# Linear attention: the dense block beside the scan in pieces of four rows at every second step, not two rows at each

## What is computed

```python
def step(s, inp):                       # one chunk of one direction
    qc, kc, vc, gc = inp
    b = cumsum(gc, axis=-2); b_last = b[..., -1:, :]
    qb = qc * exp(b); kb = kc * exp(-b)
    a = where(mask, qb @ kb.T, 0.0)
    o = qb @ s + a @ vc
    kd = kc * exp(b_last - b)
    return exp(b_last) * s + kd.T @ vc, o
# 256 context and 256 latent tokens: 8 chunks, forwards and backwards
# finish: y = (rms_norm(o_forward + o_backward) * silu(r)) @ w_out,   r = h @ w_r
```

## Time and profile before

| | |
|---|---|
| time of three runs | 2943.78, 2946.37, 2949.68 us (median 2946.37) |
| span of the profiled execution | 2941.8 us (the page gives no time beside the span) |
| TensorE busy | 2857.8 us, 97% |
| VectorE busy | 1846.1 us, 63% |
| ScalarE busy | 1144.0 us, 39% |
| GpSimd busy | 323.7 us, 11% |
| scan of layer 0, heads 0 to 2 | 819.2 to 910.8 us of the span |
| scan of layer 3, heads 0 to 2 | 2613.4 to 2703.5 us of the span |

### The profile page before, as it was taken

The page is one execution under the profiler, slowest core; times in us unless marked ns, Lnnn a source line. Parts: engine busy times, 40 slices in busy tenths (PEclk is TensorE's granted clock), DMA queues, the critical chain, the costliest instruction groups (busy, mean ns, idle before and its releaser), DMA issues.

```text
span 2941.8 us, 43541 instructions
## 1 busy us (share of the span) xinstructions
PE 2857.8 (97%) x18470; PEld 2331.1 (79%) x18470; DVE 1846.1 (63%) x2673; ACT 1144.0 (39%) x1646; POOL 323.7 (11%) x290
## 2 busy tenths in 40 slices
PE   9999999999999999999999999999999999998999
PEld 8888888997955788877667887876778878774899
DVE  4477776557465576755876676557556765546554
ACT  3345565444254422233244222344442223334443
POOL 1000003011002201111011101200111002000110
PEclk9999999999999999999999999999999999999999
DMA  8947324554211345432213444330134443221353
GB/s 295 332 136 258 129 101 158 187 187 175 99 44 40 147 158 186 172 115 101 71 45 133 182 172 158 129 112 30 44 139 176 174 156 129 102 72 44 131 185 130
DMA packets 59618, 406.76 MB, mean 138 GB/s; under 512 B 6520, under 2 KB 9848, under 8 KB 11168
## 3 DMA queue, kind: packets, MB, share of 16 engines
q1 hardware_dynamic: 58224, 399.74, 37.4%
q0 software_dynamic: 1200, 4.23, 0.5%
HBM read 402.34 MB, written 1.09 MB: 137 GB/s over the span
## 4 chain that ended last, share of the span: by engine, by line
PE 86%; DVE 8%; ACT 3%; issue 2%; POOL 1%; DVEq 0%; ACTq 0%; POOLq 0%
PE bank L626 25%; PE bank L628 24%; PE bank L627 24%; DVE xnlo L2570 1%; DVE part L2579 1%; DVE wlo L2104 1%; PE bank L732 1%; PE bank L1138 1%; PE bank L1188 1%; PE bank L1300 1%; PE bank L1282 1%; PE bank L1266 1%; PE bank L1132 1%; ACT whi L1394 1%; PE bank L1142 1%
## 5 line engine op out<-in xcount | busy, mean ns | idle before, releaser
L2104 DVE TENSOR_TENSOR wlo<-raw,whi 128x2048 fp32r<-128x2048 f32 (+2 forms) x260 | 591.4, 2274 | 410.5 <-ACT whi L1394 410.2
L1394 ACT CAST whi<-raw 128x2048 fp32r<-128x2048 f32 (+2 forms) x260 | 487.8, 1876 | 633.4 <-PE bank L628 627.6
L626 PE MATMUL bank<-xnhi,whi 128*128 128x512 f32 (+2 forms) x1760 | 657.7, 374 | 19.2 <-DVE xnlo L2570 9.8
L628 PE MATMUL bank<-xnhi,wlo 128*128 128x512 f32 (+2 forms) x1760 | 646.3, 367 | 0.0
L627 PE MATMUL bank<-xnlo,whi 128*128 128x512 f32 (+2 forms) x1760 | 644.9, 366 | 0.0
L626 PEld LDWEIGHTS bank<-xnhi,whi 128*128 128x128 f32 (+1 forms) x1760 | 332.0, 189 | 117.5 <-issue 50.0
L628 PEld LDWEIGHTS bank<-xnhi,wlo 128*128 128x128 f32 (+1 forms) x1760 | 332.3, 189 | 56.8 <-issue 0.7
L627 PEld LDWEIGHTS bank<-xnlo,whi 128*128 128x128 f32 (+1 forms) x1760 | 332.6, 189 | 54.3 <-issue 0.9
L626 PE MATMUL bank<-hidhi,whi 128*128 128x512 f32 (+1 forms) x1024 | 373.6, 365 | 0.0
L628 PE MATMUL bank<-hidhi,wlo 128*128 128x512 f32 (+1 forms) x1024 | 372.2, 364 | 0.0
L627 PE MATMUL bank<-hidlo,whi 128*128 128x512 f32 (+1 forms) x1024 | 371.3, 363 | 0.0
(11 more groups left out here) (354 smaller groups left out, 4134.2 us busy)
## 6 DMA issues: line engine op xcount, KB each, us to landing
raw<-in_wall SPq DMA_DIRECT2D x317, 1024.0 KB, 4.8
vraw<-in_wall SPq DMA_DIRECT2D x60, 1024.0 KB, 4.8
x<-in_x SPq DMA_DIRECT2D x2, 1024.0 KB, 6.8
bias<-relative_offsets POOLq DMA_DIRECT2D x2, 768.0 KB, 7.1
x<-relative_offsets POOLq DMA_DIRECT2D x2, 768.0 KB, 9.1
out<-x SPq DMA_DIRECT2D x1, 1024.0 KB, 4.8
aqk<-aqk POOLq DMA_DIRECT2D x2, 256.0 KB, 3.3
cst<-in_cst SPq DMA_DIRECT2D x1, 492.0 KB, 10.6
```

The lines of the kernel that those rows point to most:

```text
L626: mm(out, wh, xh, start=first, stop=False)
L628: return mm(out, wl, xh, start=False, stop=last)
L1394: nc.scalar.copy(b.whi[u % SPL][:, rows, cols], b.raw[pos % RAW][:, rows, cols]).then_inc(*R.made("hi_ready"))
L2104: ttn(b.wlo[u % SPL][:, rows, cols], b.raw[blocks[u] % RAW][:, rows, cols], b.whi[u % SPL][:, rows, cols], ALU.subtract).then_inc(*R.made( ...
```

## The change

`slow_unit` gives way after every fourth row, and the scan asks for a piece in steps 1, 3, 5 and 7 only:

```diff
@@ slow_unit
                 if k == KC - 1:
                     last.then_inc(*R.made("chunk_ready"))
                     g["chunks"] += 1
-                if k % 2:
+                if k % 4 == 3:
                     yield
@@ gla, end of a step
-                next(beside, None)
+                if s % 2:
+                    next(beside, None)
                 if ahead and s == 3:
                     gate_input(h + 1, 1)
```

## The result

Ten runs of the changed kernel gave 2951.39 to 2956.62 us, median 2954.83; ten of the kernel before 2943.78 to 2949.68, median 2946.32. The medians are 8.5 us apart; the ratio is 1.0027 [1.0020, 1.0035], which is 8.0 us with an interval of 5.9 to 10.3. So the change costs about 8 us. The forecast was 2955.7, in a range of 2947.5 to 2962.5. The profiled execution went from a span of 2941.8 to 2949.6, +7.8. That is near the forecast's +9.3, but it is not made up as forecast: layer 0 gave what the sum said, layer 3 did not.

The account below looks back on a forecast made before the run. TensorE's queue bounds layer 0; in layer 3 the chain passes between TensorE, VectorE and ScalarE. Layer 0's +5.1 and layer 3's +4.2 make +9.3 us; on the median 2946.37 that gives 2955.7, range 2947.5 to 2962.5.

Parts of the forecast that it names:

- -0.20 - 0.43: Layer 0: steps 4 and 5 save 0.20 us by joining pieces; L1078 of step 7 comes only its slack, 0.43, earlier.
- the price that the last head had shown: Layer 0, L1138 of step 1: with no piece in step 0 it waits 0.26 us, as in the piece-free last head.
- The step of the argument that carried it: Layer 0, step 3: L2647 stays put, so L1078 gains only its slack; step 7: L2647 shifts with TensorE, slack 0.43 us.
- One small term: Layer 0, steps 0 and 1 together: 0.26 us of wait less 0.20 for the join, about +0.06.
- the plain join: Layer 0: a piece leaving an even step saves 1.58 us, joined to the next adds 1.38; without new wait -0.20.
- The rival that had only joins: VectorE's decay rows come earlier, so only 24 joins count: -4.8 us (2941.6), or -9.6 at double worth; chance 0.10.
- The two prices of 0.70: Layer 3, each head: six more matmuls behind L1078 of steps 3 and 7 cost 0.70 us each, 4.2 in all.
- I take both as cancelling: Layer 3 at 1.2 GHz: step 3's 0.70 us becomes up to 1.40, but step 4 profits from its missing piece.
- the prediction's own last sign of being wrong: Layer 3 off by more than 3 us through the low-clock stretches; heads 0 to 2 were forecast at 94.3 us.
- the rival with the clock that comes back sooner: Layer 3: dense matmuls behind L1078 shorten the low stretches, two heads gain 2.74 us each: +3.8, 2950.2; chance 0.18.
- What was said against it: Against the sooner clock, layer 3: the idle before step 3 gets longer by about a piece.
- The deeper clock: Layer 3: second head's low stretch lengthens (+2.74 us), step 7 gains one per head (5.1): +17.1, 2963.5; chance 0.12.

Follow-up runs that it names:

- the run with steps 0 and 4 emptied: Kernel before, both layers, with the pieces of steps 0 and 4 moved to steps 1 and 5: 2941.82 us, ratio 0.9984 to the kernel before.
- the two kernels with three fillers: Kernel before and changed kernel, each with idle matmuls added in layer 3 (three in heads 0 to 2, one in last): 2937.90 and 2946.80 us.
- the run in layer 3 alone: Kernel before with the change's moved pieces in layer 3 only, layer 0 left as it was: 2947.27 us, ratio 1.0004 to the kernel before.
- the two halves: Kernel before with the change in layer 0 only, 2952.04 us (ratio 1.0016), and in layer 3 only, 2947.27 us (ratio 1.0004).
- the change with two fillers: Changed kernel with two matmuls into an unused bank at the end of step 2, layer 3, heads 0 to 2: 2948.02 us, ratio 1.0009.

## Why the prediction was right, and where it wasn't

**Layer 0 came step by step as forecast.** The starts of L1068 and L1078 in the two timelines:

| layer 0 | before | changed | moved | forecast |
|---|---|---|---|---|
| L1068 to L1078 of step 3, first head | 12.41 | 11.47 | -0.94 | -1.00 |
| the same, second head | 13.19 | 13.05 | -0.14 | -0.15 |
| L1078 of step 3 to the next L1068, first head | 2.80 | 4.17 | +1.37 | +1.38 |
| on to L1078 of step 7, first head | 12.37 | 11.72 | -0.65 | -0.20 - 0.43 |
| on to the next head's L1068, first head | 2.79 | 4.17 | +1.38 | +1.38 |

The first head is +1.16 (forecast 1.13), the second +1.92 and the third +1.93 (1.98), together 5.0 for 5.1. L1138 of step 1 waits 0.26, the price that the last head had shown. The waits at step 7 are 1.1 (1.2 was named), that at step 3 of the second head 0.97. The step of the argument that carried it, that VectorE's L2647 doesn't come earlier when TensorE does, held: in step 7 it came just as much earlier as its slack said, and not more. One small term was not consistent: 0.06 was taken off the first head's slack and not off the others'. Against the start of the head L2647 came 0.11 later in the first head (10.73 for 10.62), so it gained 0.94 and not 1.06; the total is hardly touched.

**The joins.** In the run with steps 0 and 4 emptied the half of a head with the plain join, from the gate product to L1078 of step 7, went from 12.37 to 12.14: -0.23 where -0.20 was forecast. The rival that had only joins was out from the start, since L1078 did wait.

**Layer 3: the work was sized right, the clock wrong.** The two prices of 0.70 are there at the full clock (0.69 to 0.73 and 0.66 to 0.71, 4.2 in all between the two kernels with three fillers). What failed is the sentence on the low stretches, "I take both as cancelling". In the profiled execution they don't cancel, and the prediction's own last sign of being wrong came true there: layer 3 off by more than 3 us through the low stretches (-0.5 where +4.2 was forecast; heads 0 to 2 took 89.60 us, not 94.3). By the table of layer 3, against the full-clock values of the same order of pieces, the low clock cost the kernel before 4.2 us on the way to the gate product and 6.2 on the way to step 7 (14.26 and 13.50 where 10.78 do), 10.4 in all; the changed kernel 5.5 and 0.3, 5.8 in all. So the change's 4.2 met 4.7 given back, and layer 3 came out at -0.5. In size that is the rival with the clock that comes back sooner, which I had given 0.18, in this execution: over the scans alone its +3.8 is nearer to the +4.5 of the profile (5.0 - 0.5) than the forecast's +9.3. Its mechanism isn't shown: the second head's low stretch grew from 3.4 to 6.8 us, and with the same order of pieces the run in layer 3 alone had 34 us of them. What was said against it doesn't hold either: the idle before step 3 did not get longer by a piece, it is 2.70 us in the second head in both kernels, and the new idle of 0.84 stands at step 1. What moves the low stretches stays open.

**So the total is partly luck in the profile.** The +7.8 is 5.0, -0.5 and the 3.3 outside the scans. And the profiled execution of the changed kernel was the second shortest of its ten (2951.41): its mean granted clock over the whole kernel was 0.993, where the eight longest had 0.990 or 0.991. So what the clock gave back there is not what the median holds. The medians are better evidence, since they hold many executions: +8.5, or +8.0 by the ratio, with an interval of 5.9 to 10.3. But the two halves run alone add up to +5.9 by their ratios (4.7 and 1.2, each with some 2.6 of uncertainty to either side), so how much of layer 3's 4.2 is there in the mean execution stays open, between about 1 and 4 us if both intervals are to hold. So that the median came within 1 us of the forecast is partly luck too. That the 4.2 is there at the full clock is shown by the parts of layer 3 in the two kernels with three fillers; the 8.9 us between these kernels agree.

**The deeper clock** (0.12) asked for a low stretch at step 7 of layer 3, where two waits now follow each other (0.74 for the update and 0.70 for L2648, second head). There was none in the profile of the changed kernel: what follows step 7 takes 4.29 us in both heads, as at the full clock (4.30 and 4.25 in the change with two fillers). The Trainium skill, "TensorE: Matmul & The Clock Gate", section "HAM oscillation — how this bites in real kernels", describes a kernel whose bursts of matmuls are shorter than the waits between them, and whose array is throttled again in each of these long waits. The runs here agree in part: in layer 3 of the kernel before the clock fell around the longest idle, 2.70 to 2.87 us ahead of step 3, and stayed at 1.00 when that idle was filled; in layer 0 nine new waits of 0.26 to 1.1 us left it at 1.00. But the change with three fillers had two low stretches of 3.4 us in layer 3, where no idle was longer than 1.08 us, so long waits aren't all that counts. The Trainium skill, on the same page, section "What's actually happening", says of a kernel's start that its number of slow matmuls differs from run to run. Here a stage in the middle differs likewise: the changed kernel's layer 3 and that of the run in layer 3 alone took 102.88 and 107.02 us with one and the same order of pieces.

## What to carry to other kernels

Work put beside a chain between engines is worth what stands ahead of a wait; the same work behind the wait was paid in full here, but for the one piece that covers a second wait in layer 0. So measure for each wait the slack to the releaser, compare it with the piece that is to move, and price the two sides apart: in layer 0 that gave 5.1 us where 5.0 were measured. Where the trace shows a granted clock that falls, price the work at the full clock, and hold the clock up in a pair of runs before calling a small difference a matter of order. One profile is one execution: see where its time lies among the others before reading a small difference from it.

## What the runs showed of the hardware

- Idle work shortened the kernel. Three added matmuls of 512 columns (0.86 us each) in an idle of 2.7 us, in each of three heads, and one more, kept the clock of the kernel before at 1.00 and gave back 9.7 us of layer 3; with two the clock still fell, for 20 us of layer 3, and 3.4 us of it came back.
- The low stretches of layer 3 were 3.4 to 13.7 us long, and their sum went from 20 to 34 us over the orders without fillers, and with three it was 0 (before) and 6.8 (the change); the same order had 20 us in one execution and 34 in another.
- The matmuls of 128 x 256 in the dense stage ahead of layer 3's scan ran at one of two paces with the clock at 1.00 throughout. The group of L628 in that stage, before (2531.1 to 2613.3) and then changed (2537.4 to 2620.9), with the busy time and the mean ns of one:

```profile
L628 PE MATMUL bank<-whi,xnlo 128*128 128x256 f32 x128 | 35.3, 276 | 0.0
```

```profile
L628 PE MATMUL bank<-whi,xnlo 128*128 128x256 f32 x128 | 35.8, 280 | 0.0
```

  Start to start it is 113.3 and 117.7 ns for some 280 of them in a row, 1.25 us for the stage. The same step of 1.2 us showed in the first such stage, ahead of layer 0's scan, of four experiments, ahead of any piece that was moved, so it does not come from the change; what sets it is open.
